# Hybrid decoder layer on eight cores: a hand-written planner with later landings, residual adds on Vector alone, due times per post norm, a higher charge for row-mode changes

## The reference

```python
h = swiglu(rms_norm(x, ffn1_pre_g[l]), ffn1_w_gate[l], ffn1_w_up[l], ffn1_w_down[l])
x = x + 0.5 * rms_norm(h, ffn1_post_g[l])
h = hybrid_mixer(rms_norm(x, mix_pre_g[l]), w_in[l], ..., w_out[l], l)
x = x + rms_norm(h, mix_post_g[l])
h = swiglu(rms_norm(x, ffn2_pre_g[l]), ffn2_w_gate[l], ffn2_w_up[l], ffn2_w_down[l])
x = x + 0.5 * rms_norm(h, ffn2_post_g[l])
```

## Time and profile before

| | |
|---|---|
| median of 3 runs | 2557.14 us (2553.06 to 2726.93) |
| profiled execution | 2551.94 us, its slowest core (3) spans 2550.3 us |
| spans of the eight cores | 2538.0 to 2550.3 us |
| busy on core 3 | PE 2447.3, DVE 1880.4, ACT 1402.7, POOL 423.1 us |

### The profile page before, as it was taken

How to read it: one execution, slowest core, us unless ns; L and a number is a source line. 1 busy time by engine, 2 the same in 40 slices (tenths; PEclk the granted TensorE clock), 3 DMA queues, 4 the chain that set the end, 5 groups by cost and what they waited for, 6 DMA issues and landing times.

```text
span 2550.3 us, 50061 instructions; the slowest of 8 cores (2538.0 to 2550.3 us)
## 1 busy us (share of the span) xinstructions
PE 2447.3 (96%) x16594; PEld 1275.0 (50%) x16594; DVE 1880.4 (74%) x3222; ACT 1402.7 (55%) x2039; POOL 423.1 (17%) x511
## 2 busy tenths in 40 slices
PE   6999999999999999999999999999999999999997
PEld 2444444444444466666555666544444444444466
DVE  5766986886787696555698555698778868867977
ACT  4544543653544378777686877774435435435432
POOL 1110310311121221111023111022003002100201
PEclk9999999999999999999999999999999999999998
DMA  7656866776687975435678453356345445534644
GB/s 148 119 103 139 195 114 146 159 137 135 146 177 141 222 172 95 73 57 107 152 169 212 89 94 72 85 183 202 99 146 170 133 130 155 164 112 145 198 127 163
DMA packets 136620, 356.12 MB, mean 140 GB/s; under 512 B 48304, under 2 KB 54576, under 8 KB 136368
## 3 DMA queue, kind: packets, MB, share of 16 engines
q1 hardware_dynamic: 104112, 245.07, 31.9%
q0 software_dynamic: 32256, 107.85, 26.2%
HBM read 398.83 MB, written 74.97 MB: 186 GB/s over the span
## 4 chain that ended last, share of the span: by engine, by line
PE 82%; DMA 8%; DVE 4%; issue 3%; ACT 1%; SPq 0%; DVEq 0%; POOL 0%; ACTq 0%; POOLq 0%
PE ps L979 36%; PE ps L1046 19%; PE ps L1190 8%; PE ps L1321 4%; PE ps L1143 4%; PE ps L1225 3%; PE ps L1278 3%; DVE M L746 3%; PE ps L1439 2%; DMA x<-M 2%; DMA M<-wgu 2%; DMA M<-x 1%; PE ps L1402 1%; ACT M L749 1%; DMA M<-xT 1%
## 5 line engine op out<-in xcount | busy, mean ns | idle before, releaser
L746 DVE TENSOR_TENSOR M<-M 128x1024 f16<-128x1024 f16 (+6 forms) x1649 | 959.5, 618 | 230.1 <-ACT M L749 82.1
L979 PE MATMUL ps<-M 128*128 128x512 f16 x4928 | 1080.7, 381 | 33.5 <-DVE M L746 11.3
L749 ACT ACTIVATE M<-ps 128x512 f32<-128x512 f32 (+7 forms) x955 | 706.1, 771 | 439.7 <-PE ps L1046 147.5
L979 PEld LDWEIGHTS ps<-M 128*128 128x128 f16 x4928 | 481.0, 98 | 627.6 <-issue 61.3
L749 ACT ACTIVATE M<-M 128x512 f32<-128x512 f32 (+2 forms) x640 | 386.9, 627 | 543.0 <-DVE M L746 425.3
L1046 PE MATMUL ps<-M 128*128 128x512 f16 (+1 forms) x2772 | 543.2, 357 | 5.2 <-DVE M L746 4.6
L746 POOL TENSOR_TENSOR M<-M 128x512 f32<-128x512 f32 (+2 forms) x249 | 291.0, 1172 | 1175.6 <-DVE M L874 492.6
L1046 PEld LDWEIGHTS ps<-M 128*128 128x128 f16 x2772 | 271.6, 98 | 270.1 <-issue 10.7
L746 DVE TENSOR_TENSOR M<-ps,M 128x1024 f32<-128x1024 f32 (+3 forms) x312 | 303.1, 973 | 115.8 <-PE ps L1046 69.9
L1190 PE MATMUL ps<-M 128*128 128x512 f16 x1024 | 272.8, 383 | 1.8 <-issue 1.2
L749 ACT ACTIVATE M<-ps,btab 128x1024 bf16<-128x1024 f32 x168 | 180.6, 1112 | 41.4 <-PE ps L1278 40.6
(11 more groups left out here) (50 smaller groups left out, 899.5 us busy)
## 6 DMA issues: line engine op xcount, KB each, us to landing
M<-x SPq DMA_DIRECT2D x128, 512.0 KB, 6.0
M<-wgu POOLq DMA_DIRECT2D x88, 512.0 KB, 6.3
M<-cgu SPq DMA_DIRECT2D x88, 512.0 KB, 4.1
M<-xT SPq DMA_DIRECT2D x64, 512.0 KB, 7.5
x<-M SPq DMA_DIRECT2D x64, 512.0 KB, 6.9
M<-cdn SPq DMA_DIRECT2D x40, 704.0 KB, 4.3
M<-wd POOLq DMA_DIRECT2D x32, 704.0 KB, 7.0
outT<-M SPq DMA_DIRECT2D x32, 512.0 KB, 5.8
```

Source lines behind the costliest of these rows:

```text
L746: return lambda e: e.tensor_tensor(o, a, b, op)
L749: return lambda e: e.activation(o, i, f, **k)
L979: g.pe([(lambda e, gg=gg, kc=kc, pb=pb, src=src, piece=piece, n=n: e.matmul(bank(pb + gg), src[:, gg * 512 + kc * 128:gg * 512 + (kc + 1) ...
```

## The change

It changes no arithmetic. All edits act on the planner or on what it may choose.

- The transfer time in the model is multiplied by 1.2 for DMAs from SP and by 1.15 for those from POOL, and from the second pass on `list_order` counts each landing 2.0 us later than the replay gave (`LAT_PAD`), in priorities and in the time that consumers may start. `replay` itself has the slower transfers but not the 2.0 us.
- The add to x in `post` loses its POOL alternative, in the feed-forward parts (`POOL_POST`) and after attention (`POOL_ATT`). The multiply in `finish` keeps its two (`POOL_FFN = 1`).
- In `post` of the feed-forward parts the scale, the add, the squares kept for the next norm and the stores get due times of clock + 40 + 35·tl + 4·d in place of clock + 60, with tl the tile (0 or 1) and d the chunk. The loads of x in `post` keep + 60, and `post` after attention keeps + 60 throughout.
- `MODE_PEN` goes from 0.5 to 1.0.

```diff
+SLOW = (1.2, 1.15)
+LAT_PAD = 2.0
+POST_DUE = (40.0, 35.0, 4.0)
+POOL_FFN = 1
+POOL_POST = 0
+POOL_ATT = 0
-MODE_PEN = 0.5
+MODE_PEN = 1.0
...
+        self.slack = 60.0
...
-        n = self._add(list(rd), list(wr), nom if nom is not None else self.clock + 60.0, tag)
+        n = self._add(list(rd), list(wr), nom if nom is not None else self.clock + self.slack, tag)
...
         n.pkt = (0.03 + pk * 9.4e-5) if eng == POOL else (0.012 + pk * 4.54e-5)
+        n.pkt *= SLOW[eng == POOL]
         n.work = kb * 1024.0 / (2 if eng == POOL else 1) / pk * n.pkt / 16
...
-            lat = 0.12 if n.dma is None else DMA_LAT + n.kb * 1.024 / DMA_RATE if n.lat is None else n.lat
+            lat = 0.12 if n.dma is None else DMA_LAT + n.kb * 1.024 / DMA_RATE if n.lat is None else n.lat + LAT_PAD
...
-                n.end = dfree + DMA_LAT if n.lat is None else t + n.lat
+                n.end = dfree + DMA_LAT if n.lat is None else t + n.lat + LAT_PAD
...
             for d in range(NKC):
                 y, by = Yv[:, tl, d], B_Y[tl][d]
+                g.slack = POST_DUE[0] + POST_DUE[1] * tl + POST_DUE[2] * d if half else 60.0
                 g.op([(DVE, v_stt(512), lambda e, y=y, d=d: e.scalar_tensor_tensor(
                     y, y, gains[:, gcol + d:gcol + d + 1], rst[ri], ALU.mult, ALU.mult))],
                     [by, B_rst[ri], B_gain], [by], port=True)
-                g.op([(POOL, p_tt(512), tt_(xt.ap(d), xt.ap(d), y, ALU.add)),
-                      (DVE, v_ps(512), tt_(xt.ap(d), xt.ap(d), y, ALU.add))],
+                g.op(([(POOL, p_tt(512), tt_(xt.ap(d), xt.ap(d), y, ALU.add))] if (POOL_POST if half else POOL_ATT) else []) +
+                     [(DVE, v_ps(512), tt_(xt.ap(d), xt.ap(d), y, ALU.add))],
                      [xt.buf(d), by], [xt.buf(d)], port=True)
...
+            g.slack = 60.0
```

More of the change, by code:

```diff
@@ L180 @@
 MODE_SW = 0.098
-MODE_PEN = 0.5
+MODE_PEN = 1.0
 class Node:
     __slots__ = ("i", "alts", "rd", "wr", "nom", "prio", "kb", "nbr", "pred", "succ", "np", "tab", "port", "dma",
-                 "start", "end", "eng", "alt", "occ", "tag", "rows", "pkt", "work", "lat", "fix")
+                 "start", "end", "eng", "alt", "occ", "tag", "rows", "pkt", "work", "lat", "fix", "sv")
 class Graph:
@@ L953, in finish @@
                 g.op([(ACT, a_sb(512), act_(t[:, 0:512], t[:, 0:512], AF.Silu))], bt, bt, tab="s")
-                g.op([(POOL, p_tt(512), tt_(hs(p, l), t[:, 0:512], t[:, 512:1024], ALU.mult)),
-                      (DVE, v_ps(512), tt_(hs(p, l), t[:, 0:512], t[:, 512:1024], ALU.mult))],
+                g.op(([(POOL, p_tt(512), tt_(hs(p, l), t[:, 0:512], t[:, 512:1024], ALU.mult))] if POOL_FFN else []) +
+                     [(DVE, v_ps(512), tt_(hs(p, l), t[:, 0:512], t[:, 512:1024], ALU.mult))],
                      bt, [B_H[p][l]], port=True)
```

## The result

The changed kernel took 2497.34 us (median; 2492.01 to 2498.3) against 2561.55 us for the kernel before beside it: a ratio of 0.9756 with a 95% interval of 0.972 to 0.9792, so 2.4% faster. Forecast were 2530 us and a range of 2502 to 2565.

What follows compares the result with a forecast made beforehand. PE, busy 2447.3 of 2550.3 us, was taken as the bound, with gaps from blocked ACT and DVE queues. Terms −24 − 3 + 3 − 1.5 − 5 + 5 = −25.5 us led to 2530 us, range 2502 to 2565.

Steps and rivals of the forecast that it cites:

- part 3: Post-norm due times: scale and add alternate, the first store leaves sooner at the program's end; −1.5 us, bounds 0 and 2.
- Part 1: Later assumed DMA landings shrink queue waits and PE gaps: two thirds of 35 us, −24 us, bounds 0 and 35.
- the third that was left: Share of the 35 us not counted: weight-block loads pass through five slots, so PE still waits.
- under 25: Sign of being right: ACT's waits for x fall from 53.6 to under 25 us.
- The first rival: Late weights are bound by slots and won gaps return elsewhere: about 2553 us, 2543 to 2563; chance 0.30.
- Part 2: Residual adds on Vector: 3 us gained near 1342 us, 3 us of new seam gaps, no change in sum.
- The −3 for the earlier trace: Near 1342 us, PE's 2.59 us gap behind four POOL adds and two slow DVE scales goes: 3 us gained.
- DVE turns into the bound at the seams: Extra adds on a nearly full DVE make PE wait in eight seams: about 2576 us; chance 0.12.
- Part 4: Higher row-mode charge in attention pairs score groups: 50 changes fewer, −5 us, bounds 0 and 20.
- Collisions: Shifted planner decisions meet new accidents: two new gaps, +5 us, bounds 0 and 20.
- all of it: Rival: landings give 35 us, row modes 20, no collisions: 2500 us; over 2% faster, chance 0.08.
- The tail: Program's end: DVE alternates scale and add, the last store meets less traffic; 1.5 of 4.3 us won.

Runs made afterwards that it cites:

- its offset: Kernel before with only post-norm due times 40 + 35 tl, a shift between the tiles without spacing of chunks: ratio 0.9841, 2517.6 us.
- only_defer: Kernel before with only one post-norm due time of 90 for all chunks of both tiles: ratio 0.9859, 2515.4 us.
- only_landings: Kernel before with only the slower modelled transfers and 2.0 us on each landing: 2523.4 us in one execution, before 2552.0.
- before_moved: Kernel before, its order of work held, with its 104 POOL residual adds executed on Vector in place: ratio 1.0025.
- only_vector: Kernel before, planned anew with only the residual adds restricted to Vector: ratio 1.0045, 2563.6 us.
- after_moved: Changed kernel, its order of work held, with 96 of the 192 residual adds executed on POOL: ratio 0.9804, 2500.2 us.

## Why the prediction was wrong, point by point

(In the text on record the last two groups of DVE are cited as rows 8 and the score groups as rows 9; they stand in the earlier trace rows.)

**The step that failed is part 3, the due times.** It was −1.5 us, for a store that leaves sooner at the end, with the seams counted "within part 1's two thirds". Alone it measured −24.5, its offset −37.5, and pure lateness −33.3. Beside the other parts it is still 11. The prediction names the mechanism in one clause (the later due times "take DVE's optional work out of the burst") and gives it no term of its own. What was missed is what a due time does in a strict queue. At clock + 60 the scales, adds and squares of the post norm come due while the next half's gate-up phase needs DVE most, and the planner sets them ahead of weight sums and bank additions, as the gap at 504.63 shows, where a weight sum whose block had landed 9 us before stood behind them. The rows that pointed to it were read but not costed: DVE at 98% with PE unharmed in the earlier trace rows says that DVE's load alone does not matter; then what stands ahead of the urgent operation does. The mechanism (blocked queues) was seen on ACT, where the blocker waits for a load, and not on DVE, where it is plain work that could have come later. That lateness is enough, without any spread of chunks or tiles, follows from only_defer. That the offset works by lateness alone does not follow, as said there. In the runs the due times also lower ACT's waits for x somewhat (47 to 40 us on the median core in only_defer), so the two mechanisms are not cleanly apart; but with 40 us of them left the first feed-forward part was already at 840.6 us, and with hardly any in only_landings it was at 855.8.

**Part 1, right in size, with a wrong reason for the third that was left.** −24 was forecast; −25 alone and 23 when taken out were measured. ACT's waits for x, put at "under 25", went to hardly any. The third was left for weight blocks, but DVE's waits for wgu fell from 30.7 to 2.7 us in only_landings, although the five slots stayed. What the landings did leave are the seams' gaps of 4.1 us behind DVE's own work, which is part 3's; that the share left out came out near the mark is luck. The first rival, the same waits in another place, is refuted for the landings; it is what befell the gap at 1342 us in before_moved.

**Part 2, right in its sum near zero for before's order.** The load on DVE was put at +43 us and came to 1904.2 − 1880.4 = 23.8 in after and 15.6 in before_moved: more came back than the 28 us. In before_moved the scales are 20.2 us shorter, all that they could be, and the weight sums 12.3 (773 to 744 ns; 759 in after); the rest lies in smaller groups and in overlapping ends of neighbouring operations, which busy time counts once. The multiplies stay on POOL in both kernels; what they still cost DVE was not tried. The −3 for the earlier trace rows did not show: the two scales took 1.86 us and the gap shrank to 0.89, but a longer one opened behind a late load of x. In after's order the adds' place is worth 8 to 11 us, with attention as the place, where POOL's adds reach PE. That it is for want of slack there is an inference. The Trainium skill (Perfetto Trace Analysis, Optimizing Scalar/DVE Operations) names GPSIMD as a possible relief for a full DVE and warns that the read port they share may undo it. The runs bear out the warning: the longer operations show in both orders (852 and 834 ns against 748), and their price in time in after's order, 11 us; in before's order the time moved by 0.9 us only.

**The rival "DVE turns into the bound at the seams", refuted.** In after DVE is busy 47.77, 47.29 and 48.04 of 50 us at three seams, and PE 50.00 in each. The adds could be put off past the seam, which was the point from which it decides.

**Part 4, twice the count, near the size.** 122 fewer changes in place of 50, and 6 to 10 us on the median core in place of 5; on the slowest core nothing is told apart (0.9991 [0.9956, 1.0026]). From the starts of matmuls, a change from 128 to 64 rows puts the next start 96 ns later than between two matmuls of one shape (before, core 3, 306 changes under 600 ns; 95 ns in after). For the change back the trace gives no clean price, as two matmuls run side by side ahead of it. At about 0.1 us each, as the prediction took it, 122 fewer are 12 us, of which half or more was seen.

**Collisions, +5, not found.** The orders differ by accidents of some us, though: only_vector against before_moved are 10 us apart with the same 192 adds on DVE.

**The sum.** −25.5 was forecast. With the measured values beside the other parts it is −23 − 8 − 11 − 6 = −48, with a rest of 9 that no single part holds, to −56.7. So of the 31 us that were missed, 9.5 are the due times, 8 the adds, 5 the collisions and 9 the rest: the due times are the largest of the single terms and the only one whose mechanism was given no price, but not the whole. Measured alone they would be 23. The rival "all of it" named 2500 us and so was near the time, but by 35 us of landings and 20 of row modes, which is not what happened: its nearness is luck. No case held the due times as a cause of their own.

**Readings and sums on record.** The first rival's time is 2557 − 6.5 + 5 = 2555.5, not 2553. In the stretches with PEclk 0.97 and 0.93 the clock stood at half for 6.8 and 13.7% of the 50 us, not for 3 to 7%; the work not done, 1.5 and 3.5 us, is right. Six falls were put at 11 us; core 3 has eight, and 17. In the earlier trace rows three of POOL's four operations are adds to x, the fourth has half their width, and one of the two scales alone took 4.52 us.

**The tail** went as forecast, worth about 1 us. DVE's order of time at the end, in place of eight scales and then eight adds:

```profile
2488.65 0.75 DVE L883 SCALAR_TENSOR_TENSOR M<-M,gains 128x512 f16<-128x512 f16 x1
2489.50 0.69 DVE L754 TENSOR_TENSOR M<-M 128x512 f32<-128x512 f32 x1
2490.11 0.75 DVE L883 SCALAR_TENSOR_TENSOR M<-M,gains 128x512 f16<-128x512 f16 x1
2490.96 0.69 DVE L754 TENSOR_TENSOR M<-M 128x512 f32<-128x512 f32 x1
```

From the end of the last add, 2491.65, to that of the span are 3.3 us, and were 4.3.

**What stays open.** Why the planner's order with the adds on Vector is 9 us worse alone and 8 us better in company: before_moved excludes DVE's load for the first, and after_moved shows POOL's contention with DVE for the second. Of the first, the table says where it lies: in only_vector PE's idle time ended by DVE in the first feed-forward part is 26.5 us, in before_moved, with as many adds on DVE, 16.1. Which operations of the new order cost it was not tried. Nor was it settled whether the last 9 us of the sum belong to a pair of parts or are accidents of order.

## What to carry to other kernels

In an engine's strict queue, optional work with a moderate due time is as harmful as a consumer of a late load: look not only at what an engine waits for ahead of a gap but at what it *does* there, and ask whether that could have come later. Where an edit touches a planner's due times, cost it by the urgent work it releases, not by the operations that it names. Judge each part of such a change both alone and taken out: here one part changed its sign.

## What the runs showed of the hardware

- An engine at 95 to 96% does not by itself hold up PE: 48.04 of 50 us of DVE with 50.00 of PE (after, 700 to 750).
- An add on POOL takes 1349 to 1412 ns and lengthens DVE's scales from 748 to 852 ns on average; moved to DVE it takes about 690. So 104 adds cost DVE 15.6 us of busy time net, 0.15 us each (before_moved).
- One scale on DVE took 4.52 us, in place of 0.75, while POOL ran three adds and a smaller operation back to back (before, core 3, 1341.58 us).
- The clock fell to 1.2 GHz beside gaps of 3.33 and 3.29 us in after, for 6.8 us each. Shorter gaps had falls beside them too: in before one of 2.24 us (a fall at 329.6 us), and a fall of 6.8 us at 1220.4 had gaps of 1.08 and 1.26 us as the longest of the 20 us ahead of it (core 3).
